# Half of the shift additions of block 2 on GpSimd, and the squares' constant between two halves of a subtraction

## The reference

```
def _modulate(x, shift, scale):
    return x * (1.0 + scale) + shift
...
    for l in range(DEPTH):
        ...
        n = _modulate(_rms_norm(h, norm_g[l, 0]), sh1, sc1)
        h = h + 0.5 * ga1 * _swiglu(n, ffn_w_in[l, 0], ffn_w_out[l, 0])
        n = _modulate(_rms_norm(h, norm_g[l, 1]), sh2, sc2)
        h = h + ga2 * _token_mixing(n, mix_w_in[l], ...)
        n = _modulate(_rms_norm(h, norm_g[l, 2]), sh3, sc3)
        h = h + 0.5 * ga3 * _swiglu(n, ffn_w_in[l, 1], ffn_w_out[l, 1])
    return _rms_norm(h, final_norm_g)
```

## Time and profile before

| | us |
|---|---|
| median of 3 runs | 2403.75 (2402.16 to 2404.01) |
| the profiled execution, whole time | 2406.49 |
| its span, first to last instruction | 2404.4 |
| TensorE busy in it | 2377.6 |
| VectorE busy | 1640.5 |
| ScalarE busy | 1203.3 |
| GpSimd busy | 205.7 |

### The profile page before, as it was taken

The page is one execution under the profiler, slowest core; times in us unless marked ns, Lnnn a source line. Parts: engine busy times, 40 slices in busy tenths (PEclk is TensorE's granted clock), DMA queues, the critical chain, the costliest instruction groups (busy, mean ns, idle before and its releaser), DMA issues. The chain is left out here.

```text
span 2404.4 us, 39244 instructions
## 1 busy us (share of the span) xinstructions
PE 2377.6 (99%) x16611; PEld 2169.8 (90%) x16611; DVE 1640.5 (68%) x2188; ACT 1203.3 (50%) x1446; POOL 205.7 (9%) x325
## 2 busy tenths in 40 slices
PE   8999999999999999999999999999999999999998
PEld 6999998898899999899889899889988989988997
DVE  4786888787687697778678664575555556558554
ACT  4445565434434556444443456944444445694443
POOL 2000001000200000200010001210000000121000
PEclk9999999999999999999999999999999999999999
DMA  8895556797887555689588665456656556545653
GB/s 286 291 312 170 172 164 227 265 302 233 286 306 234 167 183 167 235 285 308 182 305 306 208 172 151 141 177 210 205 181 205 191 173 174 156 139 186 211 186 111
DMA packets 371582, 514.59 MB, mean 214 GB/s; under 512 B 23728, under 2 KB 312758, under 8 KB 371408
## 3 DMA queue, kind: packets, MB, share of 16 engines
q1 hardware_dynamic: 344976, 415.80, 53.9%
q0 software_dynamic: 26432, 96.30, 11.8%
HBM read 510.90 MB, written 1.13 MB: 213 GB/s over the span
## 5 line engine op out<-in xcount | busy, mean ns | idle before, releaser
L1139 DVE TENSOR_TENSOR lo<-raw,hi 128x2048 fp32r<-128x2048 f32 x354 | 810.4, 2290 | 446.5 <-ACT hi L744 445.8
L744 ACT ACTIVATE hi<-raw 128x2048 fp32r<-128x2048 f32 (+1 forms) x389 | 742.1, 1913 | 471.3 <-PE ps L1809 190.5
L1809 PE MATMUL ps<-NH,hi 128*128 128x256 f32 x3360 | 951.3, 283 | 2.0 <-DVE arena L1270 2.0
L1809 PE MATMUL ps<-NL,hi 128*128 128x256 f32 x3360 | 942.1, 280 | 0.0
L1809 PE MATMUL ps<-NH,lo 128*128 128x256 f32 x3360 | 940.6, 280 | 0.0
L1809 PEld LDWEIGHTS ps<-NH,hi 128*128 128x128 f32 x3360 | 632.4, 188 | 16.2 <-issue 10.1
L1809 PEld LDWEIGHTS ps<-NL,hi 128*128 128x128 f32 x3360 | 633.2, 188 | 3.0
L1809 PEld LDWEIGHTS ps<-NH,lo 128*128 128x128 f32 x3360 | 634.0, 189 | 0.0
L1809 PE MATMUL ps<-hi,BH 128*128 128x512 f32 x704 | 279.9, 398 | 0.0
L1809 PE MATMUL ps<-hi,NH 128*128 128x512 f32 (+4 forms) x768 | 277.2, 363 | 0.8 <-DVE lo L1139 0.6
L1809 PE MATMUL ps<-hi,BL 128*128 128x512 f32 x704 | 277.2, 394 | 0.0
(11 more groups left out here) (318 smaller groups left out, 2038.0 us busy)
## 6 DMA issues: line engine op xcount, KB each, us to landing
raw<-in_ffn_w_in SPq DMA_DIRECT2D x176, 512.0 KB, 4.9
raw<-in_ffn_w_gu SPq DMA_DIRECT2D x174, 512.0 KB, 5.9
arena<-in_ada_w POOLq DMA_DIRECT2D x72, 1024.0 KB, 6.4
raw<-in_w_in SPq DMA_DIRECT2D x92, 512.0 KB, 4.5
raw<-in_ffn_w_down SPq DMA_DIRECT2D x88, 512.0 KB, 4.4
raw<-in_ffn_w_out SPq DMA_DIRECT2D x88, 512.0 KB, 4.4
raw<-in_mix_w_in SPq DMA_DIRECT2D x86, 512.0 KB, 4.6
raw<-in_w_branch SPq DMA_DIRECT2D x16, 512.0 KB, 4.3
```

The costliest lines, as they stand in the source:

```text
L744: last = nc.scalar.activation(dst, src, ACT.Copy)
L1139: last = nc.vector.tensor_tensor(dst, src, part.bitcast(F32), ALU.subtract)
L1809: last = nc.tensor.matmul(dst, a, b, start=start and k == 0, stop=stop and k == 2, skip_group_check=skip)
```

## The change

In the six norms whose following stage is in block 2, the shift is added to the first half of each tile by GpSimd, behind the tile's inverse root in its queue, once the first scaling is done. VectorE adds it to the second half alone. TensorE waits for GpSimd's result before the first four transposes. And in `entrance`, at all 11 boundaries, the constant for tile 1's squares is added between the two halves of the fourth low part and no longer after them.

```
@@ norm_tile, GpSimd @@
                 inverse_root(f"r2 {t}", stat[:, t, 6:7], stat[:, t, 5:6])
+                k = next((s.index + 1 for s in STAGES if s.key == key), 0)
+                if k < len(STAGES) and STAGES[k].block == 2:
+                    pool.wait_ge(shift_in, 16 * (k - STAGES_1 + 1))
+                    pool.wait_ge(dve_done, at("dve", f"scaled {t} 0"))
+                    nc.gpsimd.tensor_tensor(HN[:, t, 0:512], HN[:, t, 0:512], row_shift[:, 0:512], ALU.add).then_inc(pool_done, done("pool", f"n {t} 0"))
@@ norm, VectorE @@
                 if shifted:
                     dve.wait_ge(shift_in, 16 * (k - STAGES_1 + 1))
-                    for a, part in enumerate(parts):
-                        mine(f"scaled {t} {a}")
-                        nc.vector.tensor_tensor(HN[:, t, part], HN[:, t, part], row_shift[:, part], ALU.add).then_inc(dve_done, done("dve", f"n {t} {a}"))
+                    mine(f"scaled {t} 1")
+                    nc.vector.tensor_tensor(HN[:, t, parts[1]], HN[:, t, parts[1]], row_shift[:, parts[1]], ALU.add).then_inc(dve_done, done("dve", f"n {t} 1"))
@@ entrance, VectorE @@
-                for k in range(2):
-                    split_lo_half(s, 3, k)
+                split_lo_half(s, 3, 0)
                 mean_square_new(p, 1)
+                split_lo_half(s, 3, 1)
@@ turn_normed, TensorE @@
+                k = next((s.index + 1 for s in STAGES if s.key == key), 0)
                 for a in range(2):
-                    pe.wait_ge(dve_done, at("dve", f"n {t} {a}", key))
+                    if a == 0 and k < len(STAGES) and STAGES[k].block == 2:
+                        pe.wait_ge(pool_done, at("pool", f"n {t} 0", key))
+                    else:
+                        pe.wait_ge(dve_done, at("dve", f"n {t} {a}", key))
```

## The result

| | median us | runs |
|---|---|---|
| before | 2404.05 | 20 |
| after | 2407.61 | 20 |
| ratio | 1.0015 (95%: 1.0008 to 1.0021) | |
| the same pair once more: 2407.59 over 2403.28 | 1.0020 (1.0011 to 1.0029) | 11 and 33 |

The change costs 3.6 us in one comparison and 4.3 us in the other, 0.15 to 0.2%: slower, by little, but with 1 outside both intervals. The forecast was 2408.2 us, 0.18% more. One of the 20 executions of after, the profiled one, took 4247.54 us, with TensorE's granted clock at 0.55 over roughly its second half, so the ratio leaves it out (the median of the other 19 is 2407.43) and the trace of after is taken from the second comparison.

The account below looks back on a forecast made before the run. TensorE was taken to bound the kernel. Tile 0's 2.0 plus tile 1's 3.3 minus 5 x 0.17 for the constant gave 4.4 us, from the median 2403.75 to 2408.2 us; range 2404.5 to 2411.2.

Parts of the forecast that it names:

- The bound: TensorE busy 99% of the span; other engines matter only where it stands still, and added pauses add to the end.
- Part 1's length: At block 2 norms, GpSimd's first-half and VectorE's second-half additions block one another; a turning finishes 0.50 us later.
- T0: Start of the first of a tile's two scalings on VectorE in a block 2 norm; other times count from it.
- Rival (a): Block 2 norms: nothing blocks, the additions overlap, tile 1 loses its pauses; -4.0, 2399.8 us; chance 0.05.
- (c): Block 2 norms: a blocked instruction starts afresh at the other's end; +7.2, 2411.0 us; chance 0.08.
- (d): Block 2 norms: VectorE's remaining addition goes ahead of GpSimd's, a turning finishes 1.1 us later; +8, 2412 us; chance 0.05.
- Where it lands: Block 2 turnings: tile 0 costs 2.0 us at four, nothing behind mixers; tile 1 costs 3.3 us before the constant's gain.
- Part 2: Constant between the halves, 11 entrances: root blocked by the subtraction, tile 1's norm 0.17 us earlier at 5, nothing at 6.
- rival (b): Entrances: the root slips in ahead of the subtraction; five gain 0.70 instead of 0.17; +1.7, 2405.4 us; chance 0.12.
- roots of 1.5 us in all entrances: Expected sign of a right forecast: GpSimd's roots take 1.5 us under the fourth low part's subtraction at every entrance.

Follow-up runs that it names:

- part 1 alone: GpSimd adds the first half as in the change, but the constant stays behind the fourth low part; 2408.64 over 2403.28 us for the kernel before, +5.4.
- the run with fills: The whole change with GpSimd's addition replaced by two zero fills of the same half: 2401.88 us, -1.4 against the kernel before (0.9994).
- its run: GpSimd adds the first half for tile 1 only, constant left where it was, against the kernel before: 2406.75 over 2403.67 us, +3.1.
- tile 0's run: GpSimd adds the first half for tile 0 only, constant left where it was, against the kernel before: 2406.26 over 2403.67 us, +2.6.

## Why the prediction was right

**The bound.** TensorE is 99% busy before and after, and what was added to its pauses came out at the end: 3.9 us more of pauses, 3.6 and 4.3 us in the medians. That the intervals sum to 4.5, so near the forecast of 4.4, is in part luck: tile 1's six give 2.0 (2.4 forecast), and tile 0's 2.5 (2.0 forecast) hold 0.4 us that is not the change's. For part 1 alone the same intervals sum to 4.1 and the pauses to 4.9 more, where the median has +5.4.

**Part 1's length.** GpSimd's end at T0 + 2.57 was measured at 2.54, VectorE's at T0 + 3.12 measured at 3.09. GpSimd's additions were to take about 1.75 and took 1.65, VectorE's 1.7 and took 1.58, since both were issued 0.07 us later than I assumed while their ends were as forecast. The ends 1.16 and 0.55 after the other engine, read from two pairs in the mixer, were 1.13 and 0.55 here. Rival (a) is ruled out by these durations and by the run with fills; (c), a fresh start at the other's end, would have put VectorE's addition at T0 + 3.4; (d) was built and costs 12.8 us, so in the change GpSimd, which was issued first and had waited, went ahead, as the forecast has it.

**Where it lands.** 2.1 us for tile 0 (2.0 predicted) and 2.8 for tile 1 in the intervals of its run. The prediction's 3.3 for tile 1 contained 0.26 that tile 0 hands on behind the mixers, and 0.2 of that was seen in tile 0's run. The single interval that stands out, 1.19 us for tile 0 into 20m, covers the whole of 20f1; 0.4 us of it is a pause at a transpose of another step, which the run of part 1 alone does not have.

**Part 2.** Gains of 0.21 to 0.22 us against 0.17, VectorE idle for 0.44 us in place of 0.66 (0.4 forecast), next to nothing into 20f1 (0.04). The 0.70 us of rival (b) would have needed a root to slip in ahead, which none did. The sign "roots of 1.5 us in all entrances" failed at two of eleven, into 20m and 21m, where a smaller subtraction held the root for less; the gain is the same there.

**The size.** +4.4 us forecast, +3.6 and +4.3 measured. The chances, 0.60 for no difference and 0.38 for slower, took 0.2% as the least that can be told; the intervals turned out narrower (1.0008 to 1.0021), so a loss of 0.15% is already clear of none.

## What to carry to other kernels

Before moving work from VectorE to GpSimd, look in the trace for pairs that already overlap and read both durations. Where both engines' instructions took two operands from SBUF, they ran one after the other here, and a 0.69 us addition replaced by a 1.30 us one lengthened the chain even though GpSimd was idle for 90% of the time. What did no harm beside such an addition was a VectorE instruction with one operand in PSUM, and beside VectorE's addition a GpSimd fill, which reads nothing. When a pause of the busiest engine is to be covered by ready work, look for the next wait behind it on the same engine: at one boundary the pause only moved there, at four it went away, and over the whole kernel the medians show a third of it, with nothing at all inside their uncertainty.

## What the runs showed of the hardware

After the longest pause of all runs but for those at the kernel's first turning (2.05 us in the profile's count, GpSimd waiting for both scalings, tile 1 into 20f1) TensorE's granted clock fell. The run's windows: time, busy of PE, PEld, DVE, ACT, POOL with counts, granted clock, DMA share, GB/s:

```profile
1200.00:1203.00 3.00, 0.95 (x6) 0.47 (x5) 1.84 (x4) 0.00 (x0) 2.03 (x2) 1.00 0.01 3
1203.00:1206.00 3.00, 3.00 (x14) 2.61 (x13) 1.38 (x2) 1.20 (x2) 0.82 (x2) 0.55 0.62 233
1206.00:1209.00 3.00, 3.00 (x13) 2.40 (x12) 0.75 (x2) 0.66 (x2) 0.00 (x0) 0.88 0.44 116
1209.00:1212.00 3.00, 3.00 (x16) 2.42 (x14) 0.76 (x1) 1.94 (x2) 0.00 (x0) 1.00 0.52 132
```

0.55 is close to the lower of the two levels (1.2 of 2.4 GHz); 512-column matmuls then followed each other by 0.42 us instead of 0.23. It lasted some 3.5 us and cost about 1.5, an estimate: in this run the interval that follows, into 20m, grew by 2.7 us and its like in layer 1, into 21m, by 1.15. The pauses of 1.75 us (1187.85) and 1.79 us (1815.02) in the same run and of 1.25 us in the change left the clock at 1.00.

And a root, one element per row, that was held up by VectorE did not lengthen the VectorE instruction behind it. This is the subtraction issued beside the root of the earlier trace rows, in the kernel before:

```profile
1195.47 1.22 DVE L1150 TENSOR_TENSOR lo<-raw,hi 128x1024 fp32r<-128x1024 f32 x1
```

1.22 us is its usual time, and the root ended 0.49 us after it was issued; behind a 128x512 GpSimd addition the same subtraction takes 2.28. What decides the difference was not tried.
